# One projection panel for the decay, step, indexer-weight and key columns of the second mixer

## The reference, cut to what matters

```python
u = rmsnorm_2(h, norm1_g[l])
proj = jnp.einsum("bsd,de->bse", u, w_in[l])
(g_qkv, g_z, g_a, g_b, d_q, d_k, d_v, i_q, i_k, i_w, gate_a, gate_b) = jnp.split(proj, offsets, axis=-1)
...
beta = jax.nn.sigmoid(g_b)                                        # 8 columns
logdecay = -jnp.exp(gdn_a_log) * softplus(g_a + gdn_dt_bias)      # 8 columns
o_gdn = gated_delta_rule_chunked(gq, gk, gv, logdecay, beta)      # 8 heads of 128, chunks of 64
o_dsa = dsa_sparse_attention(d_q, d_k, d_v, i_q, layernorm_nobias(i_k, ...), i_w)
# i_k: 64 columns, one key for all 8 indexer heads; i_w: 8 columns, one weight a head
```

## Time and profile before

| | |
|---|---|
| median of 3 runs | 2515.05 us (2512.92 to 2515.93) |
| span of the profiled execution | 2513.4 us |
| time of the profiled execution outside its span | not given |
| TensorE matmul busy | 2479.0 us (99%) |
| VectorE busy | 1622.7 us (65%) |
| ScalarE busy | 1209.6 us (48%) |
| mean granted TensorE clock | 0.997 |

### The profile page before, as it was taken

The page is one execution under the profiler, slowest core; times in us unless marked ns, Lnnn a source line. Parts: engine busy times, 40 slices in busy tenths (PEclk is TensorE's granted clock), DMA queues, the critical chain, the costliest instruction groups (busy, mean ns, idle before and its releaser), DMA issues.

```text
span 2513.4 us, 37708 instructions
## 1 busy us (share of the span) xinstructions
PE 2479.0 (99%) x15346; PEld 2065.3 (82%) x15346; DVE 1622.7 (65%) x2583; ACT 1209.6 (48%) x2027; POOL 75.9 (3%) x114
## 2 busy tenths in 40 slices
PE   9999999999999999999999999999999999999998
PEld 7999888887878778878999888777776788888887
DVE  6888348866765555348887257766877655677733
ACT  6555334765546465245555246544333454444421
POOL 0111000000000000000110000000000000000000
PEclk9999999999999999999999999999999999999999
DMA  5675332222212222233775322211111112333232
GB/s 166 179 181 156 109 100 85 84 76 76 83 65 72 76 68 80 89 101 93 176 185 149 100 90 96 76 43 35 43 43 51 59 59 84 99 94 101 88 101 72
DMA packets 80525, 237.82 MB, mean 95 GB/s; under 512 B 8928, under 2 KB 10976, under 8 KB 80352
## 3 DMA queue, kind: packets, MB, share of 16 engines
q1 hardware_dynamic: 68832, 213.56, 26.5%
q0 software_dynamic: 10080, 18.35, 4.7%
q10 hardware_dynamic: 1440, 3.49, 0.4%
HBM read 233.27 MB, written 2.10 MB: 94 GB/s over the span
## 4 chain that ended last, share of the span: by engine, by line
PE 93%; DVE 4%; ACT 1%; DMA 1%; issue 1%; SPq 0%; ACTq 0%; DVEq 0%
PE bank L2311 22%; PE bank L2313 21%; PE bank L2312 21%; PE bank L2325 4%; PE bank L2327 4%; PE bank L2326 4%; PE bank L2580 2%; PE bank L2505 1%; PE bank L2411 1%; PE bank L2513 1%; PE bank L2499 1%; PE bank L2676 1%; PE bank L2486 1%; DVE hl L3094 1%; PE bank L2340 0%
## 5 line engine op out<-in xcount | busy, mean ns | idle before, releaser
L2311 PE MATMUL bank<-uR,hl 128*128 128x512 f32 x1684 | 683.4, 406 | 5.1 <-DVE uR L3105 3.2
L3094 DVE TENSOR_TENSOR hl<-raw,hl 128x1024 fp32r<-128x1024 f32 (+2 forms) x325 | 385.8, 1190 | 445.1 <-ACT hl L2725 443.8
L2313 PE MATMUL bank<-uR,hl 128*128 128x512 f32 x1684 | 658.0, 391 | 0.0
L2312 PE MATMUL bank<-uR,hl 128*128 128x512 f32 x1684 | 657.5, 390 | 0.0
L2725 ACT CAST hl<-raw 128x1024 fp32r<-128x1024 f32 (+2 forms) x325 | 329.8, 1020 | 204.8 <-PE bank L2313 196.1
L2311 PEld LDWEIGHTS bank<-uR,hl 128*128 128x128 f32 x1684 | 317.0, 188 | 93.9 <-issue 23.6
L2313 PEld LDWEIGHTS bank<-uR,hl 128*128 128x128 f32 x1684 | 316.7, 188 | 68.3
L2312 PEld LDWEIGHTS bank<-uR,hl 128*128 128x128 f32 x1684 | 317.3, 188 | 66.5 <-issue 6.0
L3088 DVE TENSOR_TENSOR hl<-raw,hl 128x1024 fp32r<-128x1024 f32 (+1 forms) x142 | 150.7, 1075 | 35.6 <-ACT hl L2721 32.4
L2325 PE MATMUL bank<-sum,hl 128*128 128x256 f32 x560 | 158.8, 284 | 2.5 <-DVE fA L3272 2.5
L2326 PE MATMUL bank<-sum,hl 128*128 128x256 f32 x560 | 158.5, 283 | 0.0
(11 more groups left out here) (521 smaller groups left out, 4337.4 us busy)
## 6 DMA issues: line engine op xcount, KB each, us to landing
raw<-in_win SPq DMA_DIRECT2D x147, 512.0 KB, 3.5
raw<-in_w SPq DMA_DIRECT2D x44, 512.0 KB, 3.5
raw<-in_w1u SPq DMA_DIRECT2D x54, 256.0 KB, 3.0
raw<-in_w2u SPq DMA_DIRECT2D x51, 256.0 KB, 3.1
raw<-in_w1g SPq DMA_DIRECT2D x22, 512.0 KB, 4.8
raw<-in_w2g SPq DMA_DIRECT2D x22, 512.0 KB, 4.5
raw<-in_w1d SPq DMA_DIRECT2D x16, 512.0 KB, 3.5
raw<-in_wssd SPq DMA_DIRECT2D x16, 512.0 KB, 3.6
```

The source lines that it names most:

```text
L2311: e.matmul(s.bank[:, :], h[:, 0, w], hi, start=s.first and q == 0, stop=False)
L2312: e.matmul(s.bank[:, :], h[:, 0, w], lo, start=False, stop=False)
L2313: i = e.matmul(s.bank[:, :], h[:, 1, w], hi, start=False, stop=s.last and q == n - 1)
L3094: e.tensor_tensor(h[:, 1, w], x[:, w], h[:, 0, w].bitcast(F), ALU.subtract).then_inc(*sig("dve_split.lo", s, i))
```

## The change

The decay, step, indexer-weight and key columns go into one panel: g_a in rows 0 to 7, g_b in 32 to 39, i_w in 40 to 47, i_k in 64 to 127. Panel 49 is gone, `win2` has 65 panels and the later ones move down by one. `boundary` still takes six panels, with panel 0 (q of head 0) as the last in place of panel 49. `narrow` no longer makes a full copy: VectorE makes the biased decay (32 rows) straight into `w` and the scaled weights into rows 64 to 95 of `nar`; ScalarE copies the key's 64 rows twice into a page `ik`, then makes the sigmoid from the panel's page. Of the scan, only 32 rows are used. A new wait in the main generator stands after the v panel of heads 4 to 7: the convolution of that v is not placed before `gdn_turn_v` of the pair two before it is.

```diff
-    "narrow": [("DVE", 0.9), ("ACT Sigmoid", 0.63), ("DVE", 0.45, "dve_gdn.copy")],
+    "narrow": [("DVE", 0.45, "dve_gdn.bias"), ("DVE", 0.45), ("ACT", 0.6, "act_idx.ik", 0), ("ACT", 0.6, "act_idx.ik", 1), ("ACT Sigmoid", 0.63)],
...
-    W2 = panels_of(d["win2"], 66)
-    boundary(T, [W2[j] for j in (32, 49, 45, 46, 47, 48)], True,
+    W2 = panels_of(d["win2"], 65)
+    boundary(T, [W2[j] for j in (32, 45, 46, 47, 48, 0)], True,
...
-        nar, w, g_ = fp.take(), fp.take(), fp.take()
-        s0 = step("narrow", b=b, nar=nar, w=w)
-        b.release(("dve_gdn.bias", s0))
-        c = yield from softplus(w, [("dve_gdn.copy", s0)], slice(0, 128))
+        nar, w, g_, ik = fp.take(), fp.take(), fp.take(), fp.take()
+        s0 = step("narrow", b=b, nar=nar, w=w, ik=ik)
+        ik.t = [("act_idx.ik", s0, 0), ("act_idx.ik", s0, 1)]
+        ikp[0] = ik
+        b.release(("dve_gdn.iw", s0), ("act_gdn.beta", s0), *ik.t)
+        c = yield from softplus(w, [("dve_gdn.bias", s0)], slice(0, 32))
...
         b = yield from ugemm(W2[16 + h])
+        yield from until(lambda: h < 4 or "turned" in S[h - h % 2 - 4])
         v = conv(b, "gconv_w", 4, 16 + h, 24, None, True, pair_page(h, "v2"), h % 2)
...
+        H["turned"] = True
...
     def project_idx():
-        x = yield from plain(49)
-        ikp[0] = x
-        yield
...
         def narrow(s):
-            nar = s.nar
-            go.wait_ge(*on("dve_gdn.bias", s))
-            activate(nar[32:64, :], nar[32:64, :], ACT.Sigmoid).then_inc(*sig("act_gdn.beta", s))
+            nar, x = s.nar, s.b
+            after(*x.t, *s.ik.after)
+            for i in range(2):
+                e.copy(s.ik[HALF[i], :], x[HALF[1], :]).then_inc(*sig("act_idx.ik", s, i))
+            after(*nar.after)
+            activate(nar[32:64, :], x[32:64, :], ACT.Sigmoid).then_inc(*sig("act_gdn.beta", s))
...
         def narrow(s):
-            nar, w = s.nar, s.w
-            after(*s.b.t, *nar.after)
-            e.tensor_scalar(nar[:, :], s.b[:, :], pc("g_bias"), None, ALU.add).then_inc(*sig("dve_gdn.bias", s))
-            go.wait_ge(*on("dve_gdn.bias", s))
-            e.tensor_scalar(nar[64:96, :], nar[64:96, :], ISC, None, ALU.mult).then_inc(*sig("dve_gdn.iw", s))
-            go.wait_ge(*on("dve_gdn.iw", s))
-            go.wait_ge(*on("act_gdn.beta", s))
-            after(*w.after)
-            e.tensor_copy(w[:, :], nar[:, :]).then_inc(*sig("dve_gdn.copy", s))
+            nar, w, x = s.nar, s.w, s.b
+            r = slice(0, 32)
+            after(*x.t, *w.after)
+            e.tensor_scalar(w[r, :], x[r, :], pc("g_bias", rows=r), None, ALU.add).then_inc(*sig("dve_gdn.bias", s))
+            after(*nar.after)
+            e.tensor_scalar(nar[64:96, :], x[32:64, :], ISC, None, ALU.mult).then_inc(*sig("dve_gdn.iw", s))
...
-    a["win2"] = blocks(np.concatenate([qkv, zz, ga, n24, gb, n24, iw, n24, ga, n24, dq, dk, dv, iq, ik, ik, gta, gtb], axis=1))
+    a["win2"] = blocks(np.concatenate([qkv, zz, ga, n24, gb, iw, gap[:, 0:16], ik, dq, dk, dv, iq, gta, gtb], axis=1))
```

More of the change, by code:

```diff
@@ L1822, in narrow_side @@
         w.release(("dve_gdn.scan", s))
-        nar.t = [("dve_gdn.nar", s), ("act_gdn.beta", s0)]
+        nar.t = [("dve_gdn.nar", s), ("act_gdn.beta", s0), ("dve_gdn.iw", s0)]
         g_.release(("dve_gdn.nar", s))
@@ L1856, in project_zg @@
         yield
-        b = yield from ugemm(W2[50 + h])
+        b = yield from ugemm(W2[49 + h])
         p = evict("tanh_ev", b, bias=hb2[:, h:h + 1])
@@ L2104, in merge_heads @@
         yield from room(6)
-        b = yield from ugemm(W2[58 + h])
+        b = yield from ugemm(W2[57 + h])
         S[h]["sg"] = evict("tanh_ev", b, bias=hb2[:, 8 + h:9 + h])
@@ L3514, in narrow_scan @@
             go.wait_ge(*on("act_gdn.gex", s))
-            e.tensor_scalar(w[:, :], w[:, :], gex, -1.0, ALU.mult, ALU.mult).then_inc(*sig("dve_gdn.rate", s))
+            one, r = slice(0, 32), slice(96, 128)
+            e.tensor_scalar(w[one, :], w[one, :], gex[one, :], -1.0, ALU.mult, ALU.mult).then_inc(*sig("dve_gdn.rate", s))
             go.wait_ge(*on("dve_gdn.rate", s))
@@ L3518, in narrow_scan @@
             after(*g.after)
-            e.tensor_tensor_scan(g[:, :], cc(1, "reset64"), w[:, :], 0.0, ALU.mult, ALU.add).then_inc(*sig("dve_gdn.scan", s))
+            e.tensor_tensor_scan(g[one, :], cc(1, "reset64", one), w[one, :], 0.0, ALU.mult, ALU.add).then_inc(*sig("dve_gdn.scan", s))
             go.wait_ge(*on("dve_gdn.scan", s))
-            r = slice(96, 128)
-            e.tensor_copy(nar[0:32, :], g[0:32, :])
-            g3 = g[r, :].rearrange("p (c l) -> p c l", l=64)
+            after(*nar.after)
+            e.tensor_copy(nar[one, :], g[one, :])
+            g3 = g[one, :].rearrange("p (c l) -> p c l", l=64)
             e.tensor_tensor(nar[r, :].rearrange("p (c l) -> p c l", l=64), g3[:, :, 63:64].broadcast_to([32, 8, 64]), g3,
@@ L3684, in ix_score @@
             for m in range(2):
-                w = iwN[:, 32 * s.i + 2 * s.h2 + m:32 * s.i + 2 * s.h2 + m + 1]
+                w = iwN[:, 32 * s.i + 8 + 2 * s.h2 + m:32 * s.i + 9 + 2 * s.h2 + m]
                 if s.h2 or m:
@@ L3921, in parameters @@
                                ("da_lambda_q1", "da_lambda_k1", "da_lambda_q2", "da_lambda_k2")], axis=1))
-    for r in (0, 96):
-        put("g_bias", z["gdn_dt_bias_2"].reshape(8, 1), slice(r, r + 8))
-        put("g_alog", z["gdn_a_log_2"].reshape(8, 1), slice(r, r + 8))
+    put("g_bias", z["gdn_dt_bias_2"].reshape(8, 1), slice(0, 8))
+    put("g_alog", z["gdn_a_log_2"].reshape(8, 1), slice(0, 8))
     put("ikg", np.concatenate([z["idx_k_norm_g_2"].reshape(64, 1)] * 2))
```

## The result

The changed kernel takes 2524.85 us, the median of four runs (2523.26 to 2525.96); the kernel before, run beside it, took 2514.50. The ratio is 1.0044, with an interval of 1.0030 to 1.0058: slower by about 10 us, where 1.6 us were predicted and 2522.8 was the top of the range.

The account below looks back on a forecast made before the run. TensorE was taken as the bound, busy 2479.0 of 2513.4 us. The terms -5.4 + 3.5 + 1.5 + 2.0 = +1.6 us, added to 2515.05, gave 2516.7 us, range 2509.8 to 2522.8.

Parts of the forecast that it names:

- The price of a panel: On TensorE: one panel's 24 matmuls go, at 0.227 us each, so -5.4 us.
- The narrow step: Narrow columns in the second mixer: softplus starts about 3 us sooner, ScalarE's copies take 1.2 us; nothing for the total.
- narrow_turn three panels later: Second mixer, after boundary's end: the narrow columns' turn moves from the 8th to the 11th panel, about 16 us later.
- The new wait: Before head 4's convolution: TensorE idles 3.5 us (0 to 6.3) behind VectorE, then low clock, 1.5 us (0 to 2.5).
- Two missing panels before the first stop: Stretch before 1696.4 us, ahead of the first stop: 7 panels instead of 9, adding 2 us TensorE idle (0 to 7).
- Everything after 1721.5 keeps its shape: Second mixer after pair 0's scan: only shifted, at no cost; wrong if later stops change length by more than 2 us.
- Slower by the wait: Wait before head 4's convolution holds 6.3 us, low clock 2.5, two missing panels 4: +7.4 us, 2522.5; chance 0.27.
- The saving arrives: narrow_turn keeps its place, the wait before head 4's convolution never binds, one panel missing: 2509.6 to 2511.6 us; chance 0.22.
- The stop moves: At pair 0's scan: two more panels fill it, its 2.25 us of idle goes; about -1 us, 2514; chance 0.06.

## Why the prediction was wrong

- **The price of a panel** (-5.4) was right: 24 matmuls are gone, and the version with head 2's z ahead gains 5.3 us.
- **The narrow step** at nothing was right: -0.6 us alone, and the interval holds no difference.
- **narrow_turn three panels later** was wrong; it moved by none. The convolution of panel 0 does stand in front of each step of the narrow chain, but one convolution more is all that each waits for (3, 5, 6 in place of 2, 4, 5), and that panel takes no TensorE time there, so counted in projected panels the turn stays. The order followed had the gates missed again and again on top of it. I had left out that TensorE itself waits for the convolutions then: 1.16 us before 1546.66. That such waits let the build's TensorE clock catch up is argued, not tested.
- **The new wait** binds, as foreseen, with no idle and no low clock there where 3.5 and 1.5 us were put down. Its mechanism was misread: the wait holds panels back for 5.4 us and the side work takes their place. The price of its length, 5.4 us by the run with a shorter wait, is paid elsewhere.
- **Two missing panels before the first stop** was right, 7 in place of 9, and its idle is 5.2 in place of 2.3 us: 2.9 where I took 2, with a clock of 0.85 that I had not put there, which is 4.5 us more (0.15 x 30.14 us of TensorE's busy time). The granted clock was 1.00 until 1691.5 and 0.50 from 1692 to 1702; idles of 0.43 and 1.23 us, before 1688.47 and 1690.99, went before the fall. The Trainium skill (TensorE: Matmul & The Clock Gate, Part 1: The HAM clock gate) has the array go to half its clock after idle; the trace agrees that idle costs more than itself.
- **Everything after 1721.5 keeps its shape** is the step that failed. To the end of pair 0's scan the sum was +1.6 us and measured -0.9; from there on it was 0 and measured +10.5 (4.5 + 7.9 - 6.5 + 4.5, rounded). Nor did the first part come out near its sum by its own terms: with idle (+3.9) and low clock (+4.5) as they were it would have been +3.0. It was shorter because side work was put off: 44 matmuls that belong to no panel are missing up to there and as many more lie behind, 32 of line 2581 (the inverse; 32 take 1.15 us in the rows) and 12 of line 2671 (the indexer's scores; 4 take 1.13 us at 1901.10). Then the main generator laid 8 panels from 1719 on and stood still from 1797 to 1817, with 2.1 us of idle; before, it laid 5 and stood still from 1773 to 1787.5, with 0.6. So only 6 panels were left to go beside side steps before the third stop, where there had been 9, and that stop began with more side work (645 matmuls, 562 before). For one, the 64 matmuls of lines 2613 and 2621 (2612 and 2620 before) were done within it, from 1895.41 on, while before they came behind it, from 1900.52 on, among panels. The later stops changed by +5.0, +7.9 and +4.5 us, where the prediction had called itself wrong from 2 us on. That the 8 panels came of other free pages is what the rule of `room` says; no trace shows the pages.
- **The rivals.** "Slower by the wait" had the sign and a part of the mechanism, but 8.8 us of its sum were idle and low clock at the wait, of which there was none. "The saving arrives" had the turn's place right and still not the time; it also had the wait never bind, and it bound. "The stop moves" came out the other way: the first stop grew from 25.0 to 35.3 us. Its sum has a term of -3.8 us that nothing gives; with the panel's -5.4 it would be -2.4, not about -1.

So the order is shown as the cause: same work in another order gives +6.6, +5.1 and +3.6 us; the saved work in the old order gives -3.5; two panels of one kind made ahead differ by 13.7 us. What is not shown is a rule by which an order could be judged beforehand. Where the stops lie doesn't give it (a late end of pair 0's scan went with a faster kernel), and the expectations of three runs were missed: the looser gate in the kernel before, and both with five pages.

## What to carry to other kernels

In a kernel whose order a planner makes, a saved piece of work is also a new plan. Price the two apart: keep the old order with the work left out, and the new order with the work kept. The forecast for the second has to reach to the end of the planned part, and the order alone was worth 3.6 to 13.7 us here, for a saving of 5.4. Then try several places for the same saving; one of them may give what the sum says, as head 2's z did. A wait can cost by what it holds back, also where no engine idles at it.

## What the runs showed of the hardware

The same 2.00 us of idle went before line 2590 at 1867.21 (after) and 1.99 before line 2589; the 32 matmuls took 1.15 us in the one and 1.97 in the other, where the clock had fallen already. In the first, the next 32 took 1.92. The length of the idle just before a group does not tell alone at which clock it runs. In the first stop of after the clock fell to 0.50 behind shorter idles, of 0.43 and 1.23 us. Two executions can differ in the clock where their work is the same: at 12 to 20 us it was 0.83 and 0.74 before and 1.00 after, 1.4 us. A copy of 64 rows by ScalarE from a page (0.63 us) cost no less than the 0.585 of a copy of 128 rows from a bank.
